# Hybrid decoder trunk on one core: mixers that begin with the value units by token block, a separate low-rank input, and a first gain spread by TensorE

## The chip, the cores and the metric

The kernel runs as one program on 1 core of a Trainium2 chip. The metric is the device time of one execution in microseconds (us). Engines are named as in the profile: PE is TensorE, DVE is VectorE, ACT is ScalarE, POOL is GpSimd and SP is the engine that issues most DMAs.

## The reference

The input `x` is 256 tokens of 1024 float32 channels. There are two layers. In words and cut down:

```python
for l in range(2):
    hn = rmsnorm(x, ln1_g[l])
    xc, gb_c, gc_c, q, k, v, g_out, a_low, gate_a, gate_b = split(hn @ w_in[l])
    y_a = gb_c * short_conv(gc_c * xc, conv_w[l])            # 512 channels, 3 taps
    log_a = log_sigmoid(a_low @ w_a2[l] + b_a[l]) / 16        # a_low has rank 16
    o = gla(q, k, v, log_a)                                   # 4 heads, chunks of 64 tokens
    y_b = rmsnorm(o, gla_norm_g[l]) * silu(g_out)
    x = x + (sigmoid(gate_a) * (y_a @ w_branch[l, 0]) + sigmoid(gate_b) * (y_b @ w_branch[l, 1])) @ w_out[l]
    h = rmsnorm(x, ln2_g[l])
    x = x + (swiglu(h) if l == 0 else moe_top2_of_8(h))       # FF 2816; experts 3584
out = rmsnorm(x, final_g)
```

## The kernel before

Each engine has its own instruction stream, written by hand, and semaphores order them.

**Weights.** SP loads a mixer's or the dense layer's weights in chunks of 1 MB (`load(c, ...)`) into a ring of six slots. A chunk is two pieces of 128x1024. ACT casts a piece into `w_hi` (L509), DVE subtracts to get `w_lo` (L707), both in rings of six pieces, and PE forms each product from three matmuls (`mm3`: hi by hi, hi by lo, lo by hi, all at L1291). `until(q)` in ACT's and DVE's streams means "split all pieces before q here"; `after(chunk)` is the same, counted in chunks of the mixer. A split of piece q waits until PE has used piece q - 6.

**A norm.** ACT squares x in four parts of 128x512 (two per block of 128 tokens, L532), DVE makes the mean squares (L725, L731), POOL the root (L1211), DVE scales by root and gain into `hn` (L752, L746), PE transposes `hn` (L1324), ACT copies the transposed values to `xt_hi` (L538) and DVE forms `xt_lo` (L773). One of the four transposed PSUM banks holds two channel groups of 128 with both token blocks, so no bank is complete before the second token block has been scaled.

**A mixer.** It has 29 chunks. Its first unit is `alow`: a whole chunk of which 16 columns are the low-rank input, multiplied as 24 matmuls of 128 columns of weights. Then come `q`, `k`, `v0`, `v1`, `xc0`, and so on, each of 48 matmuls over 256 columns. After `q`, PE multiplies the low-rank input by `w_a2` into bank 4 (L1385), and DVE, ACT, DVE turn this into the running log decays `bb` (`b_done`), on which POOL's exponents depend. After unit `ga1` PE waits for ACT's copy of `kd` (L595) and forms the state increments (L1437), then runs unit `ga2` (`win(14)`). A mixer ends with `out_piece`: the second token block's last four pieces, then `norm_transposed`.

**The start.** SP issues, in this order: both halves of x, a small part of the constants, the first gain broadcast to 128 partitions (512 KB), weight chunks 0 and 1, `small`, `w_a2`, chunk 2, the rest of the constants, the GLA gain, the router's weights, and then the other chunks. PE multiplies zeros 16 times meanwhile (`keep_warm(16)`).

Of the kernel before, what the change touches and what calls it, by code (L numbers as in the profile page):

```python
# [23 lines left out]
P = 128  # L24
# [19 lines left out]
NE = 8  # L44
# [23 lines left out]
WIN = ([("q", C_Q), ("k", C_K), ("v0", C_V), ("v1", C_V + 256), ("xc0", C_X), ("xc1", C_X + 256),  # L68
# [3 lines left out]
MIX_CHUNKS = 1 + len(WIN) + 4 + 4  # L72
MIX_PIECES = 2 * MIX_CHUNKS

UNIT_NAMES = (["alow"] + [w[0] for w in WIN] + [f"ya{n}" for n in range(4)] + [f"yb{n}" for n in range(4)]
              + [f"wo{n}" for n in range(4)])
UNIT = {name: n for n, name in enumerate(UNIT_NAMES)}

UNIT_PIECES = {"alow": 2, **{w[0]: 4 + 2 * n for n, w in enumerate(WIN)}, "ya0": 44, "ya1": 44, "ya2": 46, "ya3": 46,
               "yb0": 48, "yb1": 48, "yb2": 50, "yb3": 50, "wo0": 56, "wo1": 56, "wo2": 58, "wo3": 58}  # L80
# [19 lines left out]
MOE_AT = [R * CHUNK + HALF * p for p in range(W_HALVES)] + [CHUNK + HALF * p for p in range(10)] + [0, HALF]  # L100
# [21 lines left out]
assert sum(WIDTH) == FFE and ITEM_HALVES % RM == 0 and MOE_BASE // 2 % R == MOE_AT[W_HALVES] // CHUNK  # L122
# [35 lines left out]
def trunk(nc, x_d, ln1_d, w_in_d, w_a2_d, small_d, gla_g_d, w_br_d, w_out_d, ln2_d, fg_d, fu_d, fd_d,  # L158
          w_r_d, eg_d, eu_d, ed_d, fin_d, const_d, out_d):
    with ExitStack() as ctx:  # L160
# [40 lines left out]
        key_cols = nc.dram_tensor("key_cols", (KEYS, SEQ), F16, kind="Internal").ap()  # L201
        zeros = sb("zeros", [P, P], F32R)
# [26 lines left out]
        eb = la  # L229
        al = carve(10248, SEQ)  # L230
# [32 lines left out]
        wa2 = sb("wa2", [RANK, DEPTH, KW])  # L263
# [17 lines left out]
        gain_in = sem("gain_in")  # L281
# [59 lines left out]
        def unit_read(l, name):  # L341

            kind, n = (name, 0) if name in ("alow", "q", "k") else (name[:2], int(name[2:] or 0) if name[:1] != "v" else 0)
            if name in ("alow", "q", "k"):
                return {"alow": al_done, "q": q_done, "k": k_done}[name], l + 1
            if name[0] == "v":
                return v_done, 2 * l + int(name[1]) + 1
# [12 lines left out]
        def _(sp):  # L360
# [13 lines left out]
            def load_gain(n, src):  # L374
                if n:
                    sp.wait_ge(hn_done, 4 * n)
# [15 lines left out]
            for l in range(DEPTH):  # L392
                c = MIX_BASE[l] // 2
                if l:
                    load(c, rows(w_in_d[l], 0, KT, C_AL, 256))
# [1364 lines left out]
```

## Time and profile before

| | us |
|---|---|
| median of 3 runs | 1468.26 (1467.03 to 1469.98) |
| the profiled execution's own time | 1458.54 |
| its span, first to last instruction | 1456.7 |
| PE busy in it | 1425.8 |
| DVE, ACT, POOL busy | 479.6, 329.9, 121.4 |

The span has five stages: start and first mixer (0 to 185), dense layer (190.6 to 367.5), second mixer (373.6 to 540), routing (to 559), experts (to 1442.8), and the last norm. Busy PE time is modelled from the starts of its matmuls, so a busy PE is not one at its peak; what counts here is when PE stands still and at which clock it runs.

### The profile page before, as it was taken

What the parts mean: (1) busy time and instruction counts of PE and PEld (TensorE: products, weight loads), DVE (VectorE), ACT (ScalarE), POOL (GpSimd) and SP (SyncE); (2) the same over time, 40 slices, a digit from 0 to 9 for tenths busy, and PEclk for the clock granted to TensorE, in tenths of its full rate; (3) what the DMA queues carried; (4) which work ended last, traced back from release to release, by engine and by line L of the source; (5) the groups of instructions that cost most, each with busy time, mean ns of one, the idle gap of its engine ahead of it and who ended that gap; (6) DMA issues with size and microseconds to landing.
All of it is one profiled execution on the core that took longest, in us unless ns stands there. A gap on an engine that the chain in (4) does not pass through costs nothing.

```text
span 1456.7 us, 47280 instructions
## 1 busy us (share of the span) xinstructions
PE 1425.8 (98%) x21202; PEld 1049.9 (72%) x21202; DVE 479.6 (33%) x866; ACT 329.9 (23%) x462; POOL 121.4 (8%) x153
## 2 busy tenths in 40 slices
PE   8999999999999999999999999999999999999996
PEld 7999989999899985666666556566556556655654
DVE  6675765555776564101101101101200200200202
ACT  5554454444645431000001001001001001001001
POOL 0551000000164000000000000000000000000000
PEclk8999999999999999999999999999999999999998
DMA  9855546566466466999999999999999999999994
GB/s 321 280 175 175 174 150 199 199 215 202 150 193 206 153 256 228 406 401 408 405 392 407 406 394 405 406 393 408 407 388 408 407 389 408 407 385 406 408 387 160
DMA packets 188046, 461.22 MB, mean 317 GB/s; under 512 B 14162, under 2 KB 80000, under 8 KB 187840
## 3 DMA queue, kind: packets, MB, share of 16 engines
q1 hardware_dynamic: 186336, 453.35, 83.0%
q0 software_dynamic: 1504, 4.86, 0.9%
q8 instruction: 161, 2.64, 0.8%
q14 instruction: 45, 0.37, 0.1%
HBM read 456.06 MB, written 2.10 MB: 315 GB/s over the span
## 4 chain that ended last, share of the span: by engine, by line
PE 95%; DVE 2%; ACT 1%; issue 1%; DMA 0%; POOL 0%; SPq 0%; POOLq 0%; DVEq 0%
PE bank L1291 94%; DMA gain<-in_ln_dram 0%; PE bank L1408 0%; DVE w_lo L707 0%; POOL rs L1211 0%; PE bank L1324 0%; DVE mem L752 0%; ACT w_hi L509 0%; ACT mem L532 0%; DVE mem L957 0%; ACT xt_hi L538 0%; PE bank L1437 0%; PE bank L1501 0%; PE bank L1385 0%; DVE x L782 0%
## 5 line engine op out<-in xcount | busy, mean ns | idle before, releaser
L1291 PE MATMUL bank<-mem 128*32 128x256 f32 (+1 forms) x16240 | 880.4, 379 | 0.9 <-DVE mem L1142 0.6
L1291 PEld LDWEIGHTS bank<-mem 128*32 128x32 f32 (+1 forms) x16240 | 528.8, 110 | 349.5 <-PE bank L1291 1.2
L707 DVE TENSOR_TENSOR w_lo<-mem,w_hi 128x1024 fp32r<-128x1024 f32 x182 | 227.3, 1260 | 145.4 <-ACT w_hi L509 144.7
L1291 PE MATMUL bank<-xt_hi,w_hi 128*128 128x256 f32 x880 | 245.5, 279 | 2.6 <-DVE w_lo L707 2.1
L1291 PE MATMUL bank<-xt_lo,w_hi 128*128 128x256 f32 x880 | 243.9, 277 | 0.0
L1291 PE MATMUL bank<-xt_hi,w_lo 128*128 128x256 f32 x880 | 243.9, 277 | 0.0
L509 ACT CAST w_hi<-mem 128x1024 fp32r<-128x1024 f32 x182 | 188.9, 1050 | 186.9 <-PE bank L1291 181.9
L1291 PEld LDWEIGHTS bank<-xt_hi,w_hi 128*128 128x128 f32 x880 | 170.8, 194 | 5.1 <-issue 4.1
L1291 PEld LDWEIGHTS bank<-xt_lo,w_hi 128*128 128x128 f32 x880 | 170.8, 194 | 0.3
L1291 PEld LDWEIGHTS bank<-xt_hi,w_lo 128*128 128x128 f32 x880 | 170.7, 194 | 0.0
L1169 DVE TENSOR_TENSOR mem<-mem,bank 128x512 f32<-128x512 f32 x24 | 16.5, 688 | 388.2 <-PE bank L1291 388.2
L677 ACT ACTIVATE mem<-bank 128x512 f32<-128x512 f32 x24 | 14.3, 597 | 478.5 <-PE bank L1291 478.5
L1280 POOL DMA_INDIRECT mem<-hn_rows,mem x21 | 20.0, 951 | 680.3 <-DVE mem L1114 664.1
L1135 DVE SCALAR_TENSOR_TENSOR x<-bank,gates,x 128x256 f32<-128x256 f32 x72 | 29.1, 476 | 111.3 <-PE bank L1291 111.3
L1291 PE MATMUL bank<-w_hi,xt_hi 128*128 128x256 f32 (+1 forms) x192 | 59.7, 311 | 0.4 <-DVE xt_lo L963 0.4
L1291 PE MATMUL bank<-w_hi,xt_lo 128*128 128x256 f32 (+1 forms) x192 | 59.5, 310 | 0.0
L1291 PE MATMUL bank<-w_lo,xt_hi 128*128 128x256 f32 (+1 forms) x192 | 59.5, 310 | 0.0
L680 ACT ACTIVATE mem<-bank 128x256 f32<-128x256 f32 x8 | 3.1, 383 | 241.7 <-PE bank L1291 241.7
L1291 PE MATMUL bank<-w_hi,area 128*128 128x512 f32 x176 | 54.1, 380 | 0.0
L1173 DVE TENSOR_TENSOR mem<-mem,bank 128x256 f32<-128x256 f32 x8 | 3.4, 422 | 153.3 <-ACT mem L680 153.3
L1211 POOL TENSOR_TENSOR rs<-ms,const 128x1 f32<-128x1 f32 x10 | 7.5, 748 | 449.4 <-DVE ms L731 449.4
L1291 PE MATMUL bank<-area,w_hi 128*128 128x256 f32 x256 | 43.5, 277 | 0.0
(184 smaller groups left out, 871.3 us busy)
## 6 DMA issues: line engine op xcount, KB each, us to landing
mem<-in_eg_dram SPq DMA_DIRECT2D x224, 512.0 KB, 12.2
mem<-in_eu_dram SPq DMA_DIRECT2D x224, 512.0 KB, 14.3
mem<-in_ed_dram SPq DMA_DIRECT2D x224, 512.0 KB, 13.7
mem<-in_w_in_dram SPq DMA_DIRECT2D x42, 1024.0 KB, 5.5
mem<-in_fg_dram SPq DMA_DIRECT2D x11, 1024.0 KB, 5.3
mem<-in_fu_dram SPq DMA_DIRECT2D x11, 1024.0 KB, 5.4
mem<-in_fd_dram SPq DMA_DIRECT2D x11, 1024.0 KB, 4.9
mem<-in_w_br_dram SPq DMA_DIRECT2D x8, 1024.0 KB, 5.1
```

Source lines behind the costliest of these rows:

```text
L509: nc.scalar.copy(w_hi[:, q % H, :], src).then_inc(hi_done, 1)
L677: nc.scalar.activation(msg[:, 0:512], bank[0][:, :], ACT.Silu).then_inc(esg_done, 1)
L680: nc.scalar.activation(msg[:, 0:256].rearrange("p (g n) -> p g n", g=2), mixed(0, 0), ACT.Silu).then_inc(esg_done, 1)
L707: nc.vector.tensor_tensor(w_lo[:, q % H, :], src, w_hi[:, q % H, :].bitcast(F32), ALU.subtract).then_inc(lo_done, 1)
L1135: ins = nc.vector.scalar_tensor_tensor(out=x[:, t, cols], in0=bank[4 + q][:, 256 * t:256 * t + 256], scalar=gates[:, t, i], in1=x[:, t, co ...
L1169: nc.vector.tensor_tensor(h[:, 0:two], msg[:, 0:two], bank[2][:, :], ALU.mult).then_inc(ehf_done, 1)
L1173: nc.vector.tensor_tensor(h2, h2, mixed(0, 1), ALU.mult).then_inc(ehf_done, 1)
L1211: nc.gpsimd.tensor_tensor(rs[:, t:t + 1], ms[:, t:t + 1], const[:, K_PW:K_PW + 1], ALU.pow).then_inc(rs_done, 1)
L1280: nc.gpsimd.indirect_dma_start(fetched[:, g * QW:(g + 1) * QW], None, hn_rows[:, :], bass.IndirectOffsetOnAxis(ap=row_i[:, g:g + 1], axis= ...
L1291: return nc.tensor.matmul(out, lhs, rhs, start=first, stop=last, skip_group_check=True)
```

## The change

- **Order of units.** A mixer begins with `v0`, `v1`, then `q`, `k`. In the two value units PE first does all of token block 0 (`value_pass(..., t=0, ...)`), later all of block 1. They have banks of their own, 4 and 5.
- **Transposes by token block.** `transposes(n, t, j)` fills one bank with four channel groups of one token block, so block 0 can go on to `xt_hi` and `xt_lo` while block 1 is still being scaled. Norms 1 and 3 transpose the first half of block 0 ahead of the mixer's last out piece.
- **Low-rank input.** The host hands over its 16 columns for both layers as `w_al`. ACT and DVE split them once into `al_both` (hi beside lo), and PE forms it in 16 matmuls with 32 columns of weights (`low_rank`). A mixer has 28 chunks. `wa2` is held twice, for the hi and the lo rows, and the product by it goes to bank 6.
- **First gain.** SP loads one row of 4 KB, and PE spreads it over the partitions by two float32 matmuls with a row of ones into banks 6 and 7, from which DVE scales norm 0.
- **DMA queues.** SP now issues the gain row, x block 0, the first constants, chunk 0, x block 1, chunk 1 and further chunks. `w_al`, `small`, `w_a2` twice, the rest of the constants, the GLA gain and the router's weights go out from POOL, around its two first roots.
- **Fillers.** `keep_warm` is called with 3 and 6 matmuls at the start instead of 16, and with 3 to 8 in each of the four norms ahead of and behind the mixers.
- **Increments.** `win(14)` stands before the wait for `kd`.
- **Splits in DVE's stream.** Between the low-rank copy and the running sums DVE splits no pieces; before, it had `after(0)`, `after(1)` and `after(2)` there.

```diff
-WIN = ([("q", C_Q), ("k", C_K), ("v0", C_V), ("v1", C_V + 256), ("xc0", C_X), ...
-MIX_CHUNKS = 1 + len(WIN) + 4 + 4
+WIN = ([("v0", C_V), ("v1", C_V + 256), ("q", C_Q), ("k", C_K), ("xc0", C_X), ...
+MIX_CHUNKS = len(WIN) + 4 + 4
...
 # SP
-            for t in range(TB):
-                sp.dma_start(x[:, t, :], x_d[0, t * P:(t + 1) * P, :]).then_inc(x_in[t], 16)
+            sp.dma_start(gain[0:1, :], ln1_d[0:1, :]).then_inc(gain_in, 16)
+            sp.dma_start(x[:, 0, :], x_d[0, 0:P, :]).then_inc(x_in[0], 16)
             sp.dma_start(const[:, 0:K_BASE], const_d[:, 0:K_BASE]).then_inc(base_in, 16)
-            load_gain(0, ln1_d[0])
-            load(0, rows(w_in_d[0], 0, KT, C_AL, 256))
-            load(1, rows(w_in_d[0], 0, KT, WIN[0][1], 256))
-            sp.dma_start(small[:, :, :], small_d.rearrange("l p n -> p l n")).then_inc(mix_in, 16)
...
+            load(0, rows(w_in_d[0], 0, KT, WIN[0][1], 256))
+            sp.dma_start(x[:, 1, :], x_d[0, P:2 * P, :]).then_inc(x_in[1], 16)
+            load(1, rows(w_in_d[0], 0, KT, WIN[1][1], 256))
 # ACT, layer 0
-                    norm_squares(0, range(4))
+                    norm_squares(0, (0, 1))
+                    until(1)
+                    norm_transposed(0, (0,))
+                    until(2)
+                    norm_transposed(0, (1,))
+                    until(3)
+                    norm_squares(0, (2, 3))
+                    until(4)
+                    act.wait_ge(al_in, 16)
+                    nc.scalar.copy(al_both[:, :, :, 0:RANK], al_raw).then_inc(al_hi, 1)
+                    norm_transposed(0, (2, 3))
+                    until(H)
 # DVE, layer 0 and after it
-                    norm(0, lambda p: None)
+                    scaled(0, 0)
+                    scaled(0, 1)
+                    until(1)
+                    turned_low(0, 0)
+                    until(2)
+                    turned_low(0, 1)
+                    until(3)
+                    first_square(0, 1)
+                    mean_square(0, 1)
+                    scaled(0, 2)
+                    scaled(0, 3)
+                    until(4)
...
-                after(0)
-                after(1)
                 dve.wait_ge(z_full, l + 1)
...
-                after(2)
                 dve.wait_ge(log_done, l + 1)
 # DVE, norms 1 and 3
+                add_mixer(2)
+                scaled(n, 0)
+                scaled(n, 1)
+                until(base + MIX_PIECES + H - 3)
+                add_mixer(3)
+                turned_low(n, 0)
+                first_square(n, 1)
+                mean_square(n, 1)
+                turned_low(n, 1)
+                scaled(n, 2)
+                scaled(n, 3)
+                turned_low(n, 2)
+                turned_low(n, 3)
 # POOL
-                root(2 * l)
+                root(2 * l, (0,))
+                if l == 0:
+                    nc.gpsimd.dma_start(al_raw.rearrange("p l k r -> p (l k r)"), w_al_d[:, :]).then_inc(al_in, 16)
...
+                root(2 * l, (1,))
+                if l == 0:
+                    nc.gpsimd.dma_start(const[:, K_BASE:K_END], const_d[:, K_BASE:K_END]).then_inc(params_in, 16)
...
 # PE
+            def value_pass(q0, n, half, t, ready):
+                pe.wait_ge(tl_done, ready + 2 * t + half + 1)
+                w = pair(piece(q0 + half), lambda a: a.rearrange("p (k n) -> p k n", k=4))
+                for k in range(4):
+                    kk = 4 * half + k
+                    ins = mm3(bank[4 + n][:, t * 256:(t + 1) * 256], ...
+            def low_rank(out, l):
+                pe.wait_ge(al_lo, 1)
+                pe.wait_ge(tl_done, 8 * l + 4)
+                for kk in range(KT):
+                    for xt in (xt_hi, xt_lo):
+                        ins = mm(out[0:2 * RANK, 0:SEQ], al_both[:, l, kk, :], turns(xt[:, kk, :]), ...
...
-                norm_transposed(2 * l)
-                out = claim(l, "alow")
-                channels(out, base, 1, ready=8 * l)
+                if l:
+                    keep_warm(6, bank[3])
+                transposes(2 * l, 0, 0)
+                transposes(2 * l, 0, 1)
+                keep_warm(3, bank[3])
+                value_pass(base, 0, 0, 0, 8 * l)
+                value_pass(base, 0, 1, 0, 8 * l)
+                if l == 0:
+                    value_pass(base + 2, 1, 0, 0, 8 * l)
+                transposes(2 * l, 1, 0)
+                transposes(2 * l, 1, 1)
+                if l:
+                    value_pass(base + 2, 1, 0, 0, 8 * l)
+                value_pass(base + 2, 1, 1, 0, 8 * l)
+                low_rank(claim(l, "alow"), l)
...
+                win(14)
                 pe.wait_ge(kdt_done, l + 1)
...
-                win(14)
...
+                            if (t, half, s) == (1, 1, 1):
+                                transposes(2 * l + 1, 0, 0)
                             ins = out_piece(1, half, s, t)
...
-                norm_transposed(2 * l + 1)
+                transposes(2 * l + 1, 0, 1)
+                keep_warm(8, bank[UNIT_BANK["wo0"]])
+                transposes(2 * l + 1, 1, 0)
+                transposes(2 * l + 1, 1, 1)
+                keep_warm(4, bank[UNIT_BANK["wo0"]])
```

## Rows read from the trace of the kernel before

**Rows 1.** Page, part 1: busy time and share of each engine.

```profile
PE 1425.8 (98%) x21202; PEld 1049.9 (72%) x21202; DVE 479.6 (33%) x866; ACT 329.9 (23%) x462; POOL 121.4 (8%) x153
```

**Rows 2.** The chain that ended last: start us, us, what.

```profile
2.10 6.62 DMA gain<-in_ln_dram
...
15.66 11.12 PE bank L1291 x72
26.79 1.05 PE bank L1385 x4
27.84 59.16 PE bank L1291 x528
...
373.64 8.28 PE bank L1291 x72
...
565.16 877.61 PE bank L1291 x16328
```

**Rows 3.** Windows of PE: stretch, us, busy, granted clock, DMA share, GB/s.

```profile
11.68:21.92 10.24, 8.11 (x38) 0.51 1.11 331
...
189.18:192.59 3.41, 3.21 (x16) 0.54 0.00 0
...
370.08:373.50 3.42, 3.22 (x14) 0.54 0.00 0
...
544.16:547.57 3.41, 3.33 (x17) 0.54 0.41 165
```

**Rows 4.** Timeline, first 15 us: start, us, engine, line, instruction.

```profile
4.26 0.63 ACT L532 ACTIVATE mem<-x 128x512 f32<-128x512 f32 x1 [2.27 <-DMA x<-in_x_dram]
...
6.02 0.55 POOL L1211 TENSOR_TENSOR rs<-ms,const 128x1 f32<-128x1 f32 x1 [5.60 <-DVE ms L731]
...
12.29 1.07 ACT L538 CAST xt_hi<-bank 128x512 fp32r<-128x512 f32 x2 [5.40 <-PE bank L1324]
12.91 1.29 DVE L773 TENSOR_TENSOR xt_lo<-bank,xt_hi 128x512 fp32r<-128x512 f32 x2 [0.74 <-ACT xt_hi L538]
13.25 1.06 ACT L509 CAST w_hi<-mem 128x1024 fp32r<-128x1024 f32 x1
...
14.34 1.23 DVE L707 TENSOR_TENSOR w_lo<-mem,w_hi 128x1024 fp32r<-128x1024 f32 x1
```

**Rows 5.** SP's issues of weight chunks 0 and 1; landings of each, in that order.

```profile
2.57 0.43 SPq L368 DMA_DIRECT2D mem<-in_w_in_dram  x1
DMA to landing us min/median/max: 9.2/9.2/9.2
3.04 1.05 SPq L368 DMA_DIRECT2D mem<-in_w_in_dram  x1
DMA to landing us min/median/max: 11.9/11.9/11.9
```

**Rows 6.** Page, part 6: issues, KB each, us to landing.

```profile
mem<-in_const_dram POOLq DMA_DIRECT2D x1, 129.5 KB, 9.4
```

**Rows 7.** PE's waits over the span: us in total, times, longest.

```profile
PE bank L1437 <- ACT mem L595: 1.5, 2, 0.8
```

**Rows 8.** Timeline, end of the first mixer and norm 1.

```profile
184.58 0.38 PE L1291 MATMUL bank<-w_hi,xt_lo 128*128 128x512 f32 x1
...
184.99 0.69 DVE L782 TENSOR_TENSOR x<-x,bank 128x512 f32<-128x512 f32 x1 [0.33 <-PE bank L1291]
...
186.46 0.66 PE L1324 MATMUL bank<-const,mem 128*128 128x128 f32 x4 [1.51 <-DVE mem L752]
...
190.61 0.55 PE L1291 MATMUL bank<-xt_hi,w_hi 128*128 128x256 f32 x1 [0.20 <-DVE xt_lo L773]
```

**Rows 9.** Timeline, norm 2 and the second mixer's decays.

```profile
368.73 0.75 DVE L752 SCALAR_TENSOR_TENSOR mem<-x,rs,gain 128x512 f32<-128x512 f32 x1
...
392.06 1.28 ACT L565 ACT_TABLE_LOAD   x1
...
394.75 1.27 DVE L835 TENSOR_TENSOR_SCAN mem<-const,mem 128x256 f32<-128x256 f32 x2
```

More of the change, by code:

```diff
@@ L764, in norm @@
-                first_square(1)
-                scaled(0)
-                mean_square(1)
-                for p in range(1, 4):
-                    scaled(p)
-            def norm_transposed(n, parts):
-                for m in parts:
-                    dve.wait_ge(th_done, 4 * n + m + 1)
-                    nc.vector.tensor_tensor(xt_lo[:, 2 * m:2 * m + 2, :],
-                                            bank[4 * (n % 2) + m][:, :].rearrange("p (k t) -> p k t", k=2),
-                                            xt_hi[:, 2 * m:2 * m + 2, :].bitcast(F32), ALU.subtract
-                                            ).then_inc(tl_done, 1)
+                    g = gain[:, cols]
@@ L889, in _ @@
                 dve.wait_ge(ya_l, l + 1)
-                for chunk in (12, 14):
-                    after(chunk)
-                    scores(chunk // 2 - 6)
+                for batch in (0, 1):
+                    after(11 + 2 * batch)
+                    scores(batch)
                 for h in range(HP):
@@ L905, in _ @@
                 dve.sem_inc(st_done, 1)
-                for chunk in (17, 19):
-                    after(chunk)
-                    scores(chunk // 2 - 6)
-                after(20)
+                for batch in (2, 3):
+                    after(12 + 2 * batch)
+                    scores(batch)
+                after(19)
                 for t in range(TB):
@@ L1194, in _ @@
             output_split(2 * n_items)
-            norm(4, lambda p: residual(p, n_items, bass.ds(n_items, 1)))
+            residual(0, n_items, bass.ds(n_items, 1))
+            residual(1, n_items, bass.ds(n_items, 1))
+            first_square(4, 0)
+            mean_square(4, 0)
+            residual(2, n_items, bass.ds(n_items, 1))
+            residual(3, n_items, bass.ds(n_items, 1))
+            first_square(4, 1)
+            scaled(4, 0)
+            mean_square(4, 1)
+            for p in range(1, 4):
+                scaled(4, p)
         @block.gpsimd
@@ L1205, in step, with root @@
                 pool.wait_ge(pool_step, chain[0])
-            def root(n):
-                for t in range(TB):
+            def root(n, tokens=range(TB)):
+                for t in tokens:
                     pool.wait_ge(ms_done, 2 * n + t + 1)
@@ L1374, in win @@
                     out = claim(l, name)
[L1375 to L1388 removed]
+                    f = tokens if name[:2] == "go" else channels
+                    f(out, base + 2 * n)
+                for n in range(2, 10):
                     win(n)
```

331 lines of the change are left out of this document (187 added, 144 removed).

## The prediction

> **What bounds the kernel now.** I read the page's busy shares first [rows 1]: PE is busy 98% of the span, every other engine at most 33%. So the kernel can only shorten where PE stands still, where it runs at half clock, or where it has fewer matmuls. The chain that ended last [rows 2] says where those places are. From 565.16 to 1442.8 it is one unbroken run of PE's expert matmuls, which the change does not touch: 60% of the span is out of reach. At the front, PE's first weight matmul comes at 15.66, and the first thing waited for is the broadcast gain, which lands at 2.10 + 6.62 = 8.72. In the mixers PE is unbroken but for a few joints.
>
> Next the windows [rows 3]. The granted clock is half of full, that is the lower level of 1.2 GHz, from 11.68 to 21.92, from 189.18 to 192.59, from 370.08 to 373.50 and from 544.16 to 547.57: at the start and after each of the mixers' norms, each time after PE had stood mostly idle. Last the timelines [rows 4, 8, 9] and landings [rows 5, 6] of the four norms, since all edits but one are there.
>
> **Matmul price.** 528 matmuls of 256 columns took 59.16 us [rows 2]: 0.112 each at full clock. The first 72 took 11.12 instead of 8.06, so the half clock cost 3.06 us there.
>
> **Term 1, start and first two units.** Before, the work that both kernels share (q, k, v0, v1: 192 matmuls, and the product by `w_a2`, 1.05) ends at 27.84 + 144 x 0.112 = 43.97 [rows 2].
>
> After, I walk the streams. x block 0 is issued one slot (0.46) later, so ACT squares from about 4.7 instead of 4.26 and the root (0.55) is done at 7.0 [rows 4]; scaling two parts at 0.75 [rows 9] ends at 8.5, PE's transposes soon after. The gain is no longer late: a 4 KB row lands before x, and the float32 product by `w_a2`, two matmuls of 256 columns, took 1.05 [rows 2]: two of 512 columns are 2.1 at full and 4.2 at half clock, so banks 6 and 7 are filled at 5 to 7, ahead of the first scaling.
>
> Then the weights set the pace. Chunk 0 stands where the gain stood: x block 0, constants and 1 MB are 1.64 MB, as x, constants and the broadcast gain were, landed at 8.72. I take 8.9. Chunk 1 has 3.2 MB with and ahead of it; between the old chunk 0 (2.69 MB, landed at 2.57 + 9.2 = 11.8) and old chunk 1 (3.74 MB, at 14.9) [rows 5] this gives 13.4. ACT: cast 8.9 to 9.95 (1.06), `xt_hi` (0.54), cast to 11.5, `xt_hi`, then it waits for chunk 1, casts to 14.45, squares block 1 to 15.8, casts to 16.8, and copies the low-rank columns. DVE: `w_lo` to 11.2 (1.23), `xt_lo` to 11.85 (0.65), again `w_lo` and `xt_lo` to 13.75, third `w_lo` to 15.7, mean square, root to 16.6 to 17.1, two scalings to 18.5, fourth `w_lo` to 19.75, two `xt_lo` to 21.3. PE can begin the value passes at 11.9, 13.8 and 15.75, transpose at 17.9 and 18.6, do the fourth pass at 19.8, and start `low_rank` at T = 21.3, with 48 matmuls done. Left are 16 + 144 matmuls and 1.05: 160 x 0.112 + 1.05 = 18.95, end at 40.25. Gain 3.7. The clock decides if that holds: PE works from 11.9 almost without a break. If half clock lasts until 21.9 as before, the passes at 2.7 each and the transposes at twice their time put T at 23.4 and the gain is 1.6; if it ends by 18.5, the passes still keep up with DVE. I take 3.4. Bounds 1.6 and, if chunk 0 lands a microsecond and more earlier and T is 19.9, 5.1.
>
> **Term 2, second mixer's start.** Before, alow starts at 373.64 and the same 192 matmuls are done at 373.64 + 216 x 0.112 + 1.05 = 398.9. After, the adds and the root give the first scaling at 368.2 instead of 368.73 [rows 9]; PE transposes at 369.0, ACT and DVE follow (0.54, 0.65) and three fillers stand in front, so value pass 1 starts at 371.4 and PE does not stop again: 48 matmuls (5.4) and eight transposes, now in its stream (four took 0.66 in rows 8; I take 1.0 for eight), give T = 377.8, and the end at T + 18.95 = 396.75.
>
> One new wait: DVE no longer splits between the low-rank copy and the running sums. Piece 6 (first of k) stands behind them. From the product by `w_a2` (T + 5.5) come three DVE operations of about 0.75, two table loads of 1.28 and two activations of 0.63 on ACT, the sums 1.27, then one `w_lo` 1.23: T + 14.2, with some 0.1 at joints, while PE reaches k at T + 5.5 + 8.1 = T + 13.6. Price 0.7. In layer 0 one table load less (as far as ACT's tables stay), so none. Behind that wait stand all of PE's later units, but DVE makes a piece in 1.23 where PE takes 2.7. Gain 398.9 - 396.75 - 0.7 = 1.45, which holds only if the fillers keep the clock; bounds 0.45 (half clock until 373.5) and 2.2.
>
> **Term 3, the wait for `kd`.** It cost 0.75 per layer [rows 7]. A unit of 5.4 us now covers it; the increments come later by that much, and DVE's states have two more units of cover before pieces behind them are due. Gain 1.5, bounds 1.3 and 1.6.
>
> **Term 4, norms 1 and 3.** An out piece is six matmuls of 512 columns, 1.29 at about twice 0.112 less the fixed part, so with PE's end at 184.96 the last begins at 183.67 and the one before at 182.4. Ahead of the last PE waits for the first scaling: add at 182.45, 0.69, then 0.75, gives 183.9, and it transposes until 184.45. So PE's last product is 0.8 later than 184.96. From there the chain is the old one (add, square, root, scale, transpose, cast, subtract: 5.65 from 184.96 to 190.61 [rows 8]), so the dense layer starts 0.85 late. The fillers should keep full clock, and the half clock from 190.61 to 192.59 cost half of 2.0. Net gain 0.1 at a norm; 0.9 lost at each if the clock falls nonetheless. At norm 3 the router's 24 matmuls stand in the same place, at half clock to 547.57 [rows 3]. I take 0.1 for both together; bounds a loss of 1.8 and a gain of 0.4.
>
> **Nothing elsewhere.** Two pieces fewer per mixer for ACT and DVE are hidden under PE; 1 MB less per layer is loaded in time when PE is not waiting for data. The ring of 21 expert halves starts at another slot and is filled in the same order. The last norm has the same instructions.
>
> **Sum.** 3.4 + 1.45 + 1.5 + 0.1 = 6.5 us. The profiled execution's span becomes 1450.2 and its time 1452.0. The median of the runs is 9.7 above the profiled one, which I carry along unchanged: 1468.3 - 6.5 = 1461.8.
>
> **POOL's issues.** Seven loads now leave from POOL beside DVE's work, four of them between its two roots (7.0 and 16.1). If each waits for the longest DVE operation, 1.23 [rows 4], that is 4.9 in all and leaves 4.2 for the four themselves: the second root is in time, price 0; two microseconds late, it is the second rival's case. The Trainium skill, page SBUF — State Buffer, section "SBUF: two separate sides", speaks against this part: POOL cannot write the descriptors of its DMAs while some DVE operations hold a port that both use; it gives some 620 ns for such a DMA alone and 3100 ns overlapped. By these figures, as an estimate, four take 12.4 and the root is 3.3 late; the sum would be 3.2, not 6.5. No row here shows a load issued from POOL beside DVE's splits.
>
> **The rivals.**
> - *Data and clock come sooner* (0.20). Without the 56-byte rows of `small` in SP's way, chunks 0 and 1 land early and the clock is up by 15. Terms at their better bounds: 5.1 + 2.2 + 1.6 + 0.4 = 9.3, 1459.0.
> - *The first chunks land no sooner* (0.14): 11.8 and 14.9 as now, since the same queue binds, or POOL's issues delay the second root by 2. Either way ACT's and DVE's steps above put T at 22.9, term 1 is 1.8, the total 4.9, 1463.4.
> - *The clock falls in spite of the fillers* (0.12). Terms 1.6 + 0.45 + 1.5 - 1.8 = 1.8, 1466.5: no measurable change. For it: PE had its transposes in the gap of norm 1 and the clock fell all the same [rows 3, 8]. Against: eight fillers of 0.215 halve the gap of 5.6 in which it stood nearly idle.
> - *Slower, by POOL's late loads* (0.08, of which 0.04 decide it). DVE's running sums wait for all of the constants, GLA gain and router weights, issued by POOL from about 17 on, and every later piece stands behind this wait. They are needed at T + 10.6 = 31.9, with 0.5 spare. POOL's own load of constants took 9.4 [rows 6], old chunk 1 took 11.9 [rows 5]: with some 3 for the three issues they land at 29 to 32, just in time. Each microsecond after 32.4 is paid in full; the gain is gone at 38.9, and beyond 41.8 the kernel is measurably slower (landing at 44: 1473.4).
>
> **How the numbers follow.** The forecast has 0.46. A change under 0.2%, 2.9 us, can't be told from none. Faster holds the forecast, the first rival, nearly all of the second and part of the others: 0.80. Same: 0.15. Slower: 0.05. The range goes from a little beyond the first rival, 1457.0, to the third, 1466.5; beyond both ends I leave 0.15.
>
> **What would show it.** First weight matmul at 11 to 13 instead of 15.66, `low_rank` at 20 to 23.5; the first run of 0.5 clock shorter than 10.24; no half clock after norms 1 and 3, though PE's first matmul there is 0.85 later; the second mixer's first weight matmul 2.2 sooner after the dense layer's end; no wait of PE for `kd`; a wait of 0.7 on `w_lo` at k in layer 1. Wrong: PE waiting on `w_lo` at k by more than 2 us, or half clock at the norms.

## The result

The changed kernel takes 1459.72 us (median of 4 runs, 1459.27 to 1460.97), the kernel before, run beside it, 1468.58 (1467.03 to 1469.98): ratio 0.9942, 95% interval 0.9928 to 0.9957, so 8.5 us faster (6.3 to 10.6). The forecast was 1461.8 (1457.0 to 1466.5) and faster with 0.80. The time lies inside the range, 2 us below the forecast.

The profiled execution took 1460.97, with a span of 1459.1. That is *longer* than the span of the profile before, 1456.7. The reason is in the experts, which the change does not touch: from their first matmul to ACT's cast behind their last it was 1442.79 - 559.46 = 883.3 in the profile before, and 892.3 in the changed kernel. A second profile of the kernel before gave 891.8, and those of all kernels below 891.8 to 892.6. So the profile shown ahead of the prediction was of an unusual execution: its 1458.54 lies 5.5 below the fastest of the 61 other executions of that kernel reported below. What differs in its experts are short stops of PE's weight loads (PEld) for which the profile shows no cause, and which it calls "issue": us in total, times, longest, between the first experts and the last, in the first profile and in the repeated one.

```profile
PEld bank L1291 <- issue: 3.1, 8, 0.4
PEld bank L1291 <- issue: 11.3, 22, 1.3
```

The changed kernel has 12.0 to 12.1 us of them in its three profiles. The difference of 8.2 is nearly the 8.5 by which the stage is longer; why the stops are rare in one execution is not shown. Only the part of the first profile ahead of the experts can be compared. This table compares there, with the second profile beside the first.

| from the span's start, us | before | before, repeated | after |
|---|---|---|---|
| first weight matmul | 15.66 | 15.69 | 11.51 |
| q, k, v0, v1 and the product by `w_a2` done, layer 0 | 43.97 | 43.04 | 39.54 |
| late in the first mixer, the same stretch of 96 matmuls begins | 147.73 | 146.79 | 142.68 |
| dense layer's last matmul starts | 367.11 | 367.53 | 361.95 |
| same units done, layer 1 | 399.11 | 401.55 | 391.26 |
| that stretch in the second mixer | 502.86 | 505.30 | 494.39 |
| DVE copies the router's result | 549.23 | 551.40 | 541.06 |
| experts' first matmul | 559.46 | 561.63 | 552.83 |

(39.54 is 26.10 + 120 x 0.112, 43.04 is 26.91 + 144 x 0.112; the others of that kind alike.) 561.63 - 552.83 = 8.8 is close to the measured difference of the medians (8.9), though both profiled executions lie above their kernel's median, by 1.4 and 1.3; 6.6 is what the first profile alone shows.

The page's busy times, to be read against [rows 1]: PE is busy 9 us *more* than in the first profile, and as much as in the repeated one (1435.0): the experts' stage again.

```profile
PE 1435.2 (98%) x21219; PEld 1199.4 (82%) x21219; DVE 476.9 (33%) x864; ACT 326.5 (22%) x459; POOL 131.4 (9%) x160
```

The chain that ended last, of the changed kernel, against [rows 2]. The first thing waited for is no longer the gain but chunk 1, and behind the product by `w_a2` the long stretch begins 1.7 sooner and is 24 matmuls shorter.

```profile
3.10 9.87 DMA mem<-in_w_in_dram
...
15.64 0.57 POOL rs L1264
16.23 1.41 DVE mem L766 x2
17.64 1.15 DVE w_lo L718
...
18.92 6.12 PE bank L1355 x52
25.05 1.06 PE bank L1476 x4
26.10 56.48 PE bank L1355 x504
```

The same chain from the end of the dense layer to the second mixer's product by `w_a2`:

```profile
364.80 0.66 PE bank L1385 x4
365.45 3.33 PE bank L1355 x27
368.79 0.87 PE bank L1385 x8
369.66 7.11 PE bank L1355 x64
376.77 1.05 PE bank L1476 x4
377.82 56.48 PE bank L1355 x504
```

The start, from the timeline, against [rows 4, 5]: the gain's spread (L1449), the six fillers behind it, the first root (L1264), POOL's issues (L1271 to L1278), and the first pieces.

```profile
2.62 3.78 PE L1449 MATMUL bank<-gain,mem 1*128 1x512 f32 x4
...
6.33 2.93 PE L1355 MATMUL bank<-zeros 128*128 128x512 f32 x6
...
6.59 0.55 POOL L1264 TENSOR_TENSOR rs<-ms,const 128x1 f32<-128x1 f32 x1 [6.17 <-DVE ms L739]
...
7.14 0.76 POOL L1271 DMA_DIRECT2D mem<-in_w_al_dram  x1
...
8.04 1.05 ACT L504 CAST w_hi<-mem 128x1024 fp32r<-128x1024 f32 x1 [1.87 <-DMA mem<-in_w_in_dram]
8.45 1.06 POOL L1274 DMA_DIRECT2D wa<-in_w_a_dram  x2
...
11.51 0.38 PE L1355 MATMUL bank<-w_hi,xt_hi 128*128 128x256 f32 x1
...
12.99 1.04 ACT L504 CAST w_hi<-mem 128x1024 fp32r<-128x1024 f32 x1 [0.83 <-DMA mem<-in_w_in_dram]
...
13.59 0.38 PE L1355 MATMUL bank<-w_hi,xt_hi 128*128 128x256 f32 x1 [0.48 <-DVE xt_lo L773]
...
15.44 0.35 PE L1355 MATMUL bank<-w_hi,xt_hi 128*128 128x256 f32 x1 [0.25 <-DVE w_lo L718]
```

Chunk 0 has landed at 8.0, chunk 1 at 13.0; the three passes start at 11.5, 13.6 and 15.4.

PE's windows, against [rows 3]: full clock from 11.0 on and over the norms, and one stretch of half clock in the routing.

```profile
11.00:14.00 3.00, 2.52 (x18) 2.02 (x17) 2.28 (x3) 2.17 (x4) 0.00 (x0) 1.00 1.10 310
14.00:22.00 8.00, 7.17 (x58) 6.25 (x57) 7.22 (x11) 5.59 (x11) 2.21 (x4) 1.00 1.09 360
183.00:189.00 6.00, 4.89 (x36) 4.27 (x37) 5.05 (x7) 4.12 (x6) 0.10 (x1) 1.00 0.00 0
361.00:371.00 10.00, 9.50 (x70) 8.48 (x69) 9.06 (x17) 6.42 (x14) 1.54 (x2) 1.00 0.30 100
546.87:550.28 3.41, 3.41 (x20) 1.86 (x24) 3.14 (x23) 0.00 (x0) 0.00 (x0) 0.52 0.02 5
```

The columns are stretch, its us, busy time of PE, PEld, DVE, ACT and POOL, granted clock, DMA share, GB/s: the clock is the third number from the right. This view prints 1.00 wherever the trace has no record of the clock, and in the start the first record begins at about 11. Before it the spacing of the matmuls must be read: the six fillers above took 0.49 us each, against 0.28 at full and 0.51 at half clock for the same instruction in the routing (shown below). So PE still ran at half clock there, and came up just ahead of the first weight matmul.

### The profile page after: what moved, and what is told of

It is laid out like the page before. It is cut to its first block, busy times and chain, and to the rows that moved or that the text cites. A ratio compares the mean times of both kernels' runs of the same rounds, so it can differ in the third digit from the quotient of the medians.

```text
span 1459.1 us, 47317 instructions
## 1 busy us (share of the span) xinstructions
PE 1435.2 (98%) x21219; PEld 1199.4 (82%) x21219; DVE 476.9 (33%) x864; ACT 326.5 (22%) x459; POOL 131.4 (9%) x160
## 4 chain that ended last, share of the span: by engine, by line
PE 96%; DVE 2%; issue 1%; DMA 1%; ACT 0%; SPq 0%; POOL 0%; POOLq 0%; DVEq 0%
PE bank L1355 94%; DMA mem<-in_w_in_dram 1%; PE bank L1508 1%; DVE w_lo L718 0%; PE bank L1385 0%; DVE mem L766 0%; DVE mem L760 0%; ACT mem L527 0%; DVE mem L986 0%; DVE x L782 0%; PE bank L1602 0%; PE bank L1476 0%; PE bank L1539 0%; DVE x L1178 0%; DVE mem L979 0%
## 5 line engine op out<-in xcount | busy, mean ns | idle before, releaser
L1355 PEld LDWEIGHTS bank<-mem 128*32 128x32 f32 (+1 forms) x16240 | 679.1, 110 | 208.2 <-issue 9.1
L718 DVE TENSOR_TENSOR w_lo<-mem,w_hi 128x1024 fp32r<-128x1024 f32 x178 | 223.4, 1271 | 126.2 <-ACT w_hi L504 125.3
L1355 PE MATMUL bank<-xt_hi,w_hi 128*128 128x256 f32 x864 | 238.8, 276 | 0.0
L1355 PE MATMUL bank<-xt_lo,w_hi 128*128 128x256 f32 x864 | 237.6, 275 | 0.0
L1355 PE MATMUL bank<-xt_hi,w_lo 128*128 128x256 f32 x864 | 237.6, 275 | 0.0
L504 ACT CAST w_hi<-mem 128x1024 fp32r<-128x1024 f32 x178 | 184.3, 1048 | 171.1 <-PE bank L1355 168.0
L1355 PEld LDWEIGHTS bank<-xt_hi,w_hi 128*128 128x128 f32 x864 | 165.8, 192 | 1.3 <-issue 0.7
L1355 PEld LDWEIGHTS bank<-xt_lo,w_hi 128*128 128x128 f32 x864 | 165.8, 192 | 0.3
L1355 PEld LDWEIGHTS bank<-xt_hi,w_lo 128*128 128x128 f32 x864 | 165.9, 192 | 0.0
L1264 POOL TENSOR_TENSOR rs<-ms,const 128x1 f32<-128x1 f32 x10 | 6.4, 644 | 455.6 <-DVE ms L739 455.6
```

The lines of the kernel that those rows point to most:

```text
L504: nc.scalar.copy(w_hi[:, q % H, :], src).then_inc(hi_done, 1)
L718: nc.vector.tensor_tensor(w_lo[:, q % H, :], src, w_hi[:, q % H, :].bitcast(F32), ALU.subtract).then_inc(lo_done, 1)
L1264: nc.gpsimd.tensor_tensor(rs[:, t:t + 1], ms[:, t:t + 1], const[:, K_PW:K_PW + 1], ALU.pow).then_inc(rs_done, 1)
L1355: return nc.tensor.matmul(out, lhs, rhs, start=first, stop=last, skip_group_check=True)
```

## The experiments

Twelve runs were made, nine of them with an edit, in three groups on three chips, each beside the kernel before on the same chip. What is said of a stage comes from one profiled execution of each. The theory to be tested: the order (block 0 first) and the clock kept by the fillers carry the gain, the rest is small.

**The two kernels again.** No edit, to see how much a profile varies by itself.

> The changed kernel once more, for the spread between executions. My theory: everything up to the experts repeats to 0.1 us (first scores of layer 0 at 82.6, of layer 1 at 434.3, the router's result at 541.1), while the experts' stage, 883.3 in the profile of before and 892.3 in that of the changed kernel, differs from one execution to the next and has nothing to do with the change. Rival: the renumbered ring or the earlier start makes the experts' stage 9 us longer each time; then it is about 892 here too, and would stay about 883 in a new profile of the kernel before.

> The kernel before once more, for its experts' stage. In its first profile that stage took 883.3 us from PE's first expert matmul to its last, at a time of 1458.5, 10 below its own median; in four profiles of the new kernel and its variants it took 892.2 to 892.6. Theory (that first profile was an unusual execution): the stage takes about 893 here and the time is near 1468. Rival (the old ring position makes the stage quicker, and the long runs are long elsewhere): 883 again, with the extra time in the front part.

Measured: 1460.80 (1459.22 to 1461.12), ratio 0.9943 [0.9919, 0.9968], and 1467.86 (1466.19 to 1469.24), ratio 1.0002 [0.9989, 1.0016]. The changed kernel repeated itself to 0.2 us (experts' first matmul at 552.66). The kernel before did not: 561.63 instead of 559.46. Its windows show why, PE's busy time and then the clock:

```profile
12.40:15.90 3.50, 1.20 (x8) 0.90 1.13 333
...
187.10:194.00 6.90, 6.14 (x28) 0.51 0.14 41
371.40:378.20 6.80, 6.12 (x27) 0.51 0.00 1
545.50:548.90 3.40, 2.98 (x15) 0.51 0.08 33
```

After norms 1 and 2 the clock stayed at the lower level of 1.2 GHz for 6.8 us, where [rows 3] have 3.4 each. At the start there were two short stretches of half clock in place of one long one. So what the joints of the old kernel cost differs from execution to execution. It shows in the times as well: on these three chips the kernel before ran from 1464.1 to 1473.9 in 61 executions, its mean granted clock falling from 0.994 to 0.985 as the time rose (correlation -0.86 to -0.90 on each chip); the changed kernel's 11 repeated executions lie between 1459.2 and 1461.3, at 0.995 to 0.998.

**Block 0 not first.** All of block 1's transposes and `low_rank` go ahead of the value units, which then take both blocks at once; everything else stays.

```diff
                 transposes(2 * l, 0, 1)
                 keep_warm(3, bank[3])
-                value_pass(base, 0, 0, 0, 8 * l)
-                value_pass(base, 0, 1, 0, 8 * l)
...
                 transposes(2 * l, 1, 0)
                 transposes(2 * l, 1, 1)
...
                 low_rank(claim(l, "alow"), l)
-                value_pass(base, 0, 0, 1, 8 * l)
-                value_pass(base, 0, 1, 1, 8 * l)
+                tokens(bank[4], base)
...
```

> Undoes the value passes of token block 0 alone: PE transposes both blocks, forms the low-rank input and then does v0 and v1 as whole units. Theory (block 0's 48 matmuls fill a wait for block 1's norm): in layer 0 low_rank still starts at 20.4 and the 48 matmuls, 5.4 us, come behind it, so the first scores come at 88.0 or later instead of 82.6 (later still by up to 1.7 if the idle PE falls to half clock); in layer 1 xt_lo is complete at 371.2, low_rank could start 1.0 earlier than the 372.2 of the changed kernel, so another 4.4 are lost. In all 9.7 to 13 us slower than the changed kernel, no faster than the kernel before. Rival (the gain came from the load order, the gain row and the clock): the scores come less than 2 us later and the time stays within 3 us of the changed kernel.

Measured: 1473.46 (1471.84 to 1476.42), ratio 1.0035 [1.0023, 1.0048]: slower than before. The experts begin at 563.80, 11.1 later than with the change. Taking the order out costs 12.7 by the medians, more than the whole gain. (What is left is not the old order: it is 4.4 slower than the kernel before, and no run takes that apart.) At the start the block of 192 matmuls and the product are done at 29.79 + 144 x 0.112 = 45.92 instead of 39.3: `low_rank` waits for both blocks and nothing fills PE, and the clock is down for 6.8 there. At the second mixer another 6.1 are lost, with half clock at norm 2. The other parts (separate low-rank input, spread gain, queues) win nothing without it.

**No fillers in the norms.** `keep_warm` in the four norms removed, those of the start kept.

```diff
-                if l:
-                    keep_warm(6, bank[3])
...
-                keep_warm(8, bank[UNIT_BANK["wo0"]])
...
-                keep_warm(4, bank[UNIT_BANK["wo0"]])
```

> Leaves out the filler matmuls in the norms 1, 2 and 3 (8 and 4, 6 and 3, 8 and 4), keeps those at the start. Theory (fillers keep the clock): half clock comes back at the norms for some 3.4 us each; PE's first real matmul comes up to 0.86 earlier at norms 1 and 3 and 0.65 at norm 2, but 1.0 to 1.7 is lost behind it, so 0 to 1 us per norm slower, 0.5 to 3 in all. Rival (the fillers only stand in the way): no half clock appears and each norm is 0.6 to 0.9 faster, 2.0 to 2.4 in all.

Measured: 1466.35 (1463.55 to 1466.82), ratio 0.9976 [0.9963, 0.9989]; experts at 558.00, 5.3 later than with fillers. PE's windows at norm 1, at half clock where the changed kernel has 1.00:

```profile
185.00:189.00 4.00, 3.36 (x16) 0.50 0.00 0
189.00:193.00 4.00, 4.00 (x33) 0.86 0.73 234
```

3.7 of the 5.3 are there by the second mixer's product by `w_a2` (381.35 against 377.61), 1.6 come at norm 3. By the medians the fillers are worth 5.5 us, and the times of the two kernels do not overlap (1463.55 is the lowest without, 1461.12 the highest with them). I had expected 0.5 to 3, with some 3.4 of half clock at each norm; at norm 1 it lasted twice that.

**No fillers at the start.** The six ahead of the first transposes and the three behind them removed in layer 0.

```diff
-            keep_warm(6, bank[3])
             pe.wait_ge(base_in, 16)
...
-                keep_warm(3, bank[3])
+                if l:
+                    keep_warm(3, bank[3])
```

> Leaves out the 6 filler matmuls behind the spread of the gain and the 3 behind the first transposes in layer 0. Theory (the start keeps full clock because PE is never idle long): the clock falls near 11.7 as in the kernel before and the four value passes run at half speed, 2.7 instead of 1.35 each; T, the start of low_rank, moves from 20.4 to about 22 to 23.5, so the first scores come 1.5 to 3 later. Rival (transposes and value passes are work enough): no half clock, scores at 82.6 as before or 0.3 sooner.

Measured: 1460.39 (1459.49 to 1461.11), ratio 0.9942 [0.9921, 0.9963]: the changed kernel's time. Yet the clock did fall short. The first record of the clock begins at 15.0 here, and up to there the weight matmuls stand 0.213 us apart, which is half clock; behind it they stand 0.111 apart. The changed kernel has 0.111 from its first weight matmul on.

```profile
12.23 0.42 PE L1355 MATMUL bank<-w_lo,xt_hi 128*128 128x256 f32 x1
12.45 0.42 PE L1355 MATMUL bank<-w_hi,xt_lo 128*128 128x256 f32 x1
...
15.14 0.28 PE L1355 MATMUL bank<-w_hi,xt_hi 128*128 128x256 f32 x1
15.25 0.28 PE L1355 MATMUL bank<-w_lo,xt_hi 128*128 128x256 f32 x1
...
16.49 0.35 PE L1355 MATMUL bank<-w_hi,xt_hi 128*128 128x256 f32 x1 [0.18 <-DVE w_lo L718]
```

So the fillers bring the clock up 4 us earlier, and it is worth nothing here: the third pass, at 16.49, waits for `w_lo` of chunk 1 and not for PE. The chain began 1.04 later (27.14 against 26.10), as much as chunk 1 landed later after its issue, 10.91 against 9.87. Whether half clock would cost something with chunk 1 as early as in the changed kernel, whose third pass began at 15.44, is not shown.

**Fillers alone, in the old kernel.** If the fillers are worth 5.5, are they all of it? Six matmuls of zeros ahead of norm 2's transposes; in norms 1 and 3 six between the blocks' transposes and four behind. (The changed kernel has 9 at norm 2 and 12 at norms 1 and 3.)

```diff
+                if n == 2:
+                    for _ in range(6):
+                        mm(bank[3][:, :], zeros[:, :], zeros[:, 0:1].to_broadcast([P, 512]), True, True)
                 for t in range(TB):
+                    if n % 2 and t == 1:
+                        for _ in range(6):
+                            mm(bank[UNIT["wo0"] % 4][:, :], zeros[:, :], ...
...
+                if n % 2:
+                    for _ in range(4):
+                        mm(bank[UNIT["wo0"] % 4][:, :], zeros[:, :], ...
```

> The kernel before with fillers alone: six matmuls of zeros ahead of norm 2's transposes, and in norms 1 and 3 six between the two token blocks' transposes and four behind them; all else in the old order. Theory (the fillers are worth what they were in the changed kernel because they keep the clock, whatever the order of the work): the dense layer and the units behind norm 2 run at full clock, no half clock at 189, 370 or 544; the dense layer's end 1.7 to 3.4 sooner than in the repeated kernel before, the experts' first matmul 3 to 5 sooner than its 561.6, time 1463.5 to 1465.5. Rival (the fillers only pay together with the new order, since in the old one they stand in front of transposes on the critical chain, each late by up to 1): no gain, 1466 to 1469.

Measured: 1468.76 (1466.43 to 1469.52), ratio 0.9998 [0.9986, 1.0011]: nothing, as the rival had it. PE's timeline at norm 1:

```profile
183.12 0.69 DVE L782 TENSOR_TENSOR x<-x,bank 128x512 f32<-128x512 f32 x1 [0.33 <-PE bank L1291]
...
185.56 0.66 PE L1330 MATMUL bank<-const,mem 128*128 128x128 f32 x4 [0.31 <-DVE mem L752]
...
185.97 2.67 PE L1291 MATMUL bank<-zeros 128*128 128x512 f32 x6
...
188.43 1.63 PE L1330 MATMUL bank<-const,mem 128*128 128x128 f32 x8
...
190.77 0.27 PE L1291 MATMUL bank<-xt_hi,w_hi 128*128 128x256 f32 x1
```

The clock falls at 186.2, just as the fillers begin, so six of them take 2.4 instead of 1.3, and block 1's transposes are queued behind them. The dense layer begins 190.77 - 183.12 = 7.65 after the last add, in the repeated kernel before 189.86 - 184.05 = 5.8: the fillers cost 1.85 and won 2.0 back later (dense layer done 183.3 after that add, there 183.5). At norm 2 the clock held, worth 2.3 against the repeated profile. At norm 3 it held too, but half clock came in the gather behind the routing, and took 1.5:

```profile
555.13 4.32 PE L1291 MATMUL bank<-mem,area 128*32 128x256 f32 x48
```

Full clock makes it 2.80. In the new order block 0's first transposes stand *ahead* of the mixer's last piece and the fillers directly behind it, while DVE still scales block 1; by this reading, that is what lets them cover the gap instead of lengthening it.

**The gain as a broadcast again,** behind the constants in SP's order, without the spread by PE.

```diff
-            sp.dma_start(gain[0:1, :], ln1_d[0:1, :]).then_inc(gain_in, 16)
...
+            sp.dma_start(gain[:, :], ln1_d[0].partition_broadcast(P)).then_inc(gain_in, 16)
...
-                    g = bank[6 + p % 2][:, :]
+                    g = gain[:, cols]
```

> Undoes the first gain alone in the changed kernel: SP broadcasts 512 KB behind the small constants, DVE scales from that, and 6 fillers stand where the spread stood. Theory (the gain was late, and its 512 KB stand ahead of chunk 0): the gain lands at about 7, chunk 0 half a megabyte later, 9.5 instead of 8.0, chunk 1 at 14.5 instead of 13.0; DVE's path after chunk 1 sets T, so the scores come 1.5 later, 84.0. Rival (the row and the spread gave most of the 4.4 of the start): 3 or more later, because the first scaling waits.

Measured: 1460.89 (1460.55 to 1462.48), ratio 0.9951 [0.9935, 0.9967]. Chunk 1 lands 11.45 after its issue instead of 9.87, and the chain is 1.7 to 1.9 late from there on (27.79 against 26.10). Experts at 554.60, 1.8 to 1.9 later. In this trace the 508 KB ahead of the chunks cost that much, and not the gain's own landing. But the profiled execution (1462.14) is one of the three slower ones of eight, five lie at 1460.55 to 1460.89, and chunk 1's landing varies by 1.4 without this edit (9.50 to 10.91 in the kernels that keep POOL's loads). So the spread is worth up to 1.9; by the medians, 0.1 to 1.2, no gain is shown.

**Small loads on SP.** The seven loads that the change gave to POOL go back to SP, `w_al`, `small`, `w_a2` behind chunk 1 and the others between later chunks.

```diff
             load(1, rows(w_in_d[0], 0, KT, WIN[1][1], 256))
+            sp.dma_start(al_raw.rearrange("p l k r -> p (l k r)"), w_al_d[:, :]).then_inc(al_in, 16)
+            sp.dma_start(small.rearrange("p l n -> p (l n)"), small_d[:, :]).then_inc(mix_in, 16)
...
-                    nc.gpsimd.dma_start(al_raw.rearrange("p l k r -> p (l k r)"), w_al_d[:, :]).then_inc(al_in, 16)
-                    nc.gpsimd.dma_start(small.rearrange("p l n -> p (l n)"), small_d[:, :]).then_inc(mix_in, 16)
```

> Puts the seven small loads back on SP's queue in their new packed form, four behind chunk 1 and three behind chunk 2; everything else as in the changed kernel. Theory (what hurt was small's 56-byte rows, 4.6 us of issue, not the queue): issues of 0.5 each hold chunk 2 and chunk 3 back by 2 and 3.5 us, which have the time; scores at 82.5 plus or minus 0.3. Rival (SP's queue is what the front waits for): q or k wait for their chunks, scores 1 us or more later.

Measured: 1459.05 (1458.0 to 1460.12), ratio 0.9945 [0.9927, 0.9964]. Chain at 25.39 instead of 26.10 or 25.89. Chunk 1 landed 9.0 after its issue here, and that alone can account for it. Which queue takes the loads is worth at most 0.7, in SP's favour.

**`win(14)` behind the increments again.**

```diff
-                win(14)
                 pe.wait_ge(kdt_done, l + 1)
...
                 ins.then_inc(inc_full, 1)
+                win(14)
```

> Puts win(14) back behind the state increments. Theory: PE waits 0.75 for kd in each layer again, so the end of the first mixer comes 0.65 later (159.5) and the experts 1.3 later; the time rises by about 1.3. Rival (the kd wait is gone anyway because ACT has fewer pieces to split ahead of the copy): no wait, no difference.

Measured: 1461.61 (1460.04 to 1462.02), ratio 0.996 [0.9947, 0.9973]. The wait of [rows 7] is back, in PE's waits of this kernel:

```profile
PE bank L1538 <- ACT mem L604: 1.5, 2, 0.8
```

The chain is 0.66 late after mixer 1 and 1.30 after mixer 2. Both mixers pay alike.

**Fillers in the routing,** and the changed kernel a third time beside it. Two matmuls of zeros more ahead of the five of L1718 to L1722, two behind them.

```diff
-            keep_warm(12)
+            keep_warm(14)
...
                              ).then_inc(rank_full, 1)
+            keep_warm(2)
```

> The changed kernel with two fillers more ahead of the router's transposes and two behind the matmul of the ranks. Theory: the half clock from 546.87 to 550.28 came because PE does nearly nothing in the routing; with the fillers it stays full, the four matmuls of zeros and the gather come 1.5 sooner in all, the experts' first matmul at 551.2 instead of 552.7, time 1459.3. Rival: PE is idle elsewhere in the routing and the same stretch of half clock appears again, as it did in the changed kernel: 552.7 and 1460.8, or a few tenths later by the fillers themselves.

> The changed kernel once more, beside the others. Theory: 1459.5 to 1461, experts' first matmul at 552.7, one run of half clock at 547 to 550. Rival: should the fall of the clock in the routing be a matter of the execution and not of the kernel, it is missing this time, and the experts start at 551.2.

Measured: 1459.47 (1459.28 to 1459.71), ratio 0.9932 [0.9915, 0.9949], and 1459.96 (1459.34 to 1461.29), ratio 0.9937 [0.9924, 0.9951]. The third profile of the changed kernel had *no* half clock in the routing, as its rival said. First its fillers and gather, then the same lines of the first profile of the changed kernel:

```profile
546.88 1.11 PE L1355 MATMUL bank<-zeros 128*128 128x512 f32 x4 [0.56 <-DVE keys L1096]
547.92 2.80 PE L1355 MATMUL bank<-mem,area 128*32 128x256 f32 x48
```

```profile
546.83 2.04 PE L1355 MATMUL bank<-zeros 128*128 128x512 f32 x4 [0.56 <-DVE keys L1096]
548.80 3.44 PE L1355 MATMUL bank<-mem,area 128*32 128x256 f32 x48
```

Experts follow at 551.35 and at 552.83: 1.5 us, which some executions pay and some don't (four of the nine profiles of the changed kernel and its variants that leave the routing alone). With the fillers experts begin at 551.12, and the four times lie within 0.4. The gain on the median, 0.5, is smaller than the measurement can tell; that the fillers prevent the fall in every execution is not shown by four.

**All three together:** small loads on SP, the routing fillers, and in layer 0 block 1's squares and scalings ahead of the third piece's split.

```diff
-                    until(3)
                     first_square(0, 1)
                     mean_square(0, 1)
                     scaled(0, 2)
                     scaled(0, 3)
                     until(4)
```

> The changed kernel with the small loads back on SP, the two pairs of routing fillers, and block 1's squares and scalings ahead of the split of the third piece in layer 0. Theory: the three add up. The small loads on SP gave 0.5 at the chain piece behind the product by w_a2 (25.4), block 1's earlier scaling brings its transposes and the low-rank product up to 0.7 sooner but the third pass up to 1 later (net 0 to 0.5), the routing 1.5: experts' first matmul at 550.0 to 550.6, time 1458.0 to 1458.8. Rival: PE in the start is bound by when chunk 1 lands, so that only the order of waits changes, and small_on_sp's 550.5 and 1459.05 had the routing's gain in it already: 1459.

Measured: 1460.74 (1459.9 to 1461.74), ratio 0.9942 [0.9928, 0.9955]: no better. The clock was full from 12.4 on, but the front lost 1.5 against the small loads alone (26.89 against 25.39). Its chain:

```profile
15.86 1.15 DVE w_lo L726
...
17.14 1.58 PE bank L1352 x12
...
21.25 4.59 PE bank L1352 x40
```

In PE's stream the third pass stands ahead of block 1's transposes. Split late, it holds up the very transposes whose input came sooner. An order changed on DVE and ACT alone only moves the wait to PE. Neither half of this kernel beat the changed one by more than a measurement can tell (1459.05 and 1459.47 against 1459.7 to 1460.8).

## Why the prediction was right, and where it was not

| step | forecast | against the first profile | against the repeated one |
|---|---|---|---|
| term 1, start | 3.4 | 4.4 | 3.5 |
| term 3, `kd`, two mixers | 1.5 | 1.2 | 1.2 |
| term 4, norm 1 | about 0.05 | 0.1 | 1.5 |
| term 2, second mixer's start | 1.45 | 2.7 | 4.7 |
| term 4, norm 3 | about 0.05 | -0.3 | -0.6 |
| routing (not in the sum) | 0 | -1.5 | -1.5 |
| sum | 6.5 | 6.6 | 8.8 |

Each entry is the growth of the difference from one line of the first table to the next.

- **Term 1** held, stream by stream. Chunk 0 came at 8.0 (forecast 8.9), chunk 1 at 13.0 (13.4), the passes at 11.5, 13.6, 15.4 (11.9, 13.8, 15.75), `low_rank` at 20.46 (21.3). So the end came 0.7 before the forecast 40.25. The open question of the step, the clock, came out well: full from the first weight matmul, so neither 3.06 nor any part of it was paid, and the 0.3 kept back for it was too much. The fillers brought the clock up by then. Without them half clock lasted until 15.0 and no time was lost either, which is the forecast's own condition: "if it ends by 18.5, the passes still keep up with DVE".
- **POOL's issues** took 0.76 us for the first and 0.51 to 0.59 for the others, with DVE's scalings and `w_lo` beside them, and landed 5.3 to 6.6 later. The second root ran at 15.64, directly on DVE's mean square. So the price of 0 held: POOL went from one issue to the next without a wait. The Trainium skill, page SBUF — State Buffer, section "SBUF: two separate sides", has a longer time for a DMA from POOL under a DVE operation. The second root was not late by it; whether the landings were longer no run tells, since none has these loads without DVE's work beside them, nor which of DVE's operations here hold the shared port. The rival *slower, by POOL's late loads* died the same way: the constants landed 6.6 after 16.16, at 22.8, and the last of the three loads at 23.5, more than seven before the running sums at 31.1.
- **Term 2** was mis-sized. The first pass began 365.95 - 362.17 = 3.8 after the dense layer's matmuls, as forecast (4.0), but the wait of 0.7 for `w_lo` at k never came. ACT loaded the first of its two tables while it still waited for DVE (its operand came at 379.5), so one load of 1.28 lay under that wait, and the later pieces were split in time. The rest of the 1.3 is smaller: `low_rank` came 10.0 after the dense layer instead of 10.5, and the kernel before finished the shared units at 399.11, not 398.9. The changed kernel's timeline there:

```profile
377.40 1.28 ACT L569 ACT_TABLE_LOAD   x1
...
382.83 1.27 DVE L864 TENSOR_TENSOR_SCAN mem<-const,mem 128x256 f32<-128x256 f32 x2
...
384.02 3.89 DVE L718 TENSOR_TENSOR w_lo<-mem,w_hi 128x1024 fp32r<-128x1024 f32 x3
```

  I had put all of the decays' operations in one chain; a table load needs no data, and belongs beside it.
- **Term 3** gave 0.62 per mixer in place of 0.75: the wait went, and the run with `win(14)` late gave 0.66 and 1.30 of it back, so it is this edit's alone. Why it is 0.1 short of 0.75 is not explained.
- **Term 4** against the first profile is as forecast at norm 1, and 0.35 worse at norm 3. Its reading of the price was not: "0.9 lost at each if the clock falls nonetheless" took the half clock of one profile as *the* half clock. In the second profile it lasted twice as long at norm 1 and norm 2, and without the norms' fillers the kernel loses 5.5.
- **Where the step from profile to median was weak:** a single profile was taken for the kernel, and the median's 9.7 above it were "carried along unchanged". Of these, 8.5 to 9 belong to the experts' stage of that one execution, and carrying them was right, since both medians have them. What can't be carried along is what the change itself removes, half clock at the joints, which the kernel before pays differently from execution to execution. With the usual experts' stage the first profile's execution would have taken 1467.0 to 1467.5, some 1.3 below the median of 1468.6. The changed kernel's profiled execution lies 1.3 above its median and paid 1.5 in the routing, which not all pay. These two, about half each, lead from the 6.6 of the profiles to the 8.9 between the medians. That the first is clock is likely, as the times rise when the mean clock falls, but not shown for that execution. Nor is the miss clear of noise: the interval of 6.3 to 10.6 contains 6.5. The rival *data and clock come sooner* (1459.0) is thus near in its number, but its mechanism, chunks landing earlier, is only a part of it.
- **Luck:** that the first profile's sum is 6.6 against a forecast of 6.5. Terms 1 and 2 gave 2.3 more than forecast; term 3, norm 3 and the routing, which was not in the sum, took 2.1 of it back.
- **The rival with the clock falling in spite of the fillers** was right about one place, a place that I had not priced: the routing, where 1.5 are paid in two of the changed kernel's three profiles.

Open: why PE's unexplained stops were rare in one execution, so that the experts took 883.3. It was not seen again, and no run was aimed at it.

## What to carry to other kernels

When a norm over two token blocks stands between stretches of dense matmuls, let PE begin with the block that is ready and with a unit that can take blocks one at a time, and put fillers only where PE is truly idle: ahead of a transpose that was already due they cost here what they saved. Fillers that bring the clock up in a stretch that waits for data anyway save nothing. Profile the kernel before twice before you sum against one execution, and compare stage by stage, since an untouched stage can differ by more than the change is worth. When one engine's order is changed, walk the stream of every engine behind it: the old order there decides.

## What the runs showed of the hardware

- TensorE's granted clock at a joint differs between executions of one kernel: 3.4 or 6.8 us at half rate after norms 1 and 2 of the kernel before, one stretch or none in the routing of the changed one. With work spread over the joints the mean clock rose (0.985 to 0.994 before, 0.995 to 0.998 after) and the times drew together, from 9.8 us between extremes in 61 executions to 2.1 in 11.
- In the start PE began at half clock. With three and six fillers around the gain's spread and three behind the first transposes it was at full clock from the first weight matmul (11.5 and 11.8 in three profiles); without the last nine it stood still from 9.9 to 11.9 and reached full clock at 15.0.
- The experts' stage of 892 us has some 20 stops of PE's weight loads, up to 1.3 us each and 11 to 12 us in all, for which the profile shows no cause; one of the fourteen profiled executions had 8 of them, 3.1 us.
- With 508 KB more on SP's queue ahead of it chunk 1 landed 11.45 after its issue. Without them it landed 9.5 to 10.9 after it, over otherwise like starts, and PE's chain moved by as much (1.25 between 9.66 and 10.91).
- Seven loads issued from POOL beside DVE's work took 0.5 to 0.8 us each to issue.
